# Twenty of the 31 taps of one channel half of a depthwise convolution computed on GpSimd instead of VectorE

## What is computed

```python
glu  = a * sigmoid(b)                 # a, b: two of the parts of h @ w_in, 256 channels each
conv = _dwconv(glu, conv_a_w, conv_a_b)   # 31 taps, padding 15 on both sides
y    = silu(layer_norm(conv, ln_a_g, ln_a_b))
```

## Time and profile before

| what | us |
|---|---|
| median of three runs | 2552.96 |
| the profiled execution | 2552.17 |
| its span on the core | 2550.5 |
| TensorE busy | 2430.3 (95% of the span) |
| VectorE busy | 1620.2 (64%) |
| ScalarE busy | 991.7 (39%) |
| GpSimd busy | 30.6 (1%) |
| mixer loop of layer 0, taps of line 2119 | 1646.6 to 1738.9 |
| mixer loop of layer 1, taps of line 2119 | 2237.2 to 2311.0 |

### The profile page before, as it was taken

How to read it: one execution, slowest core, us unless ns; L and a number is a source line. 1 busy time by engine, 2 the same in 40 slices (tenths; PEclk the granted TensorE clock), 3 DMA queues, 4 the chain that set the end, 5 groups by cost and what they waited for, 6 DMA issues and landing times. The chain is left out here.

```text
span 2550.5 us, 30749 instructions
## 1 busy us (share of the span) xinstructions
PE 2430.3 (95%) x12146; PEld 1941.0 (76%) x12146; DVE 1620.2 (64%) x2607; ACT 991.7 (39%) x1532; POOL 30.6 (1%) x64
## 2 busy tenths in 40 slices
PE   7999999999999999999999998998999999878997
PEld 3878877866686888886668996766788888757997
DVE  7776665444476886766457676487775454576664
ACT  2322322255523322224445444465331232455543
POOL 0000000010000000000000000000000000000000
PEclk9999999999999999999899999999999999988999
DMA  8355445531341444442314552211335443222653
GB/s 319 102 210 188 163 145 185 219 144 68 147 171 62 153 174 159 148 148 84 119 39 143 191 179 92 82 62 54 121 135 198 157 173 124 79 83 83 199 179 120
DMA packets 95802, 357.15 MB, mean 140 GB/s; under 512 B 10969, under 2 KB 11353, under 8 KB 93353
## 3 DMA queue, kind: packets, MB, share of 16 engines
q1 hardware_dynamic: 93082, 339.37, 38.3%
q0 software_dynamic: 2576, 15.82, 1.7%
HBM read 349.90 MB, written 5.24 MB: 139 GB/s over the span
## 5 line engine op out<-in xcount | busy, mean ns | idle before, releaser
L1546 DVE TENSOR_TENSOR w_lo<-raw,w_hi 128x1024 fp32r<-128x1024 f32 (+1 forms) x456 | 543.4, 1209 | 354.3 <-ACT w_hi L1026 353.9
L1026 ACT ACTIVATE w_hi<-raw 128x1024 fp32r<-128x1024 f32 (+1 forms) x456 | 461.6, 1041 | 539.5 <-PE PS L527 528.9
L527 PE MATMUL PS<-h_hi,w_hi 128*128 128x512 f32 (+1 forms) x1528 | 524.5, 343 | 19.4 <-DVE h_lo L1898 9.2
L527 PE MATMUL PS<-h_lo,w_hi 128*128 128x512 f32 (+1 forms) x1528 | 521.2, 341 | 0.0
L527 PE MATMUL PS<-h_hi,w_lo 128*128 128x512 f32 (+1 forms) x1528 | 520.5, 341 | 0.0
L527 PEld LDWEIGHTS PS<-h_hi,w_hi 128*128 128x128 f32 x1528 | 287.7, 188 | 64.3 <-issue 12.9
L527 PEld LDWEIGHTS PS<-h_hi,w_lo 128*128 128x128 f32 x1528 | 287.7, 188 | 35.9
L527 PEld LDWEIGHTS PS<-h_lo,w_hi 128*128 128x128 f32 x1528 | 287.9, 188 | 34.7 <-issue 0.2
L527 PE MATMUL PS<-hid_hi,w_hi 128*128 128x512 f32 (+1 forms) x864 | 292.3, 338 | 0.0
L527 PE MATMUL PS<-hid_lo,w_hi 128*128 128x512 f32 (+1 forms) x864 | 292.2, 338 | 0.0
L527 PE MATMUL PS<-hid_hi,w_lo 128*128 128x512 f32 (+1 forms) x864 | 292.2, 338 | 0.0
(11 more groups left out here) (341 smaller groups left out, 3440.4 us busy)
## 6 DMA issues: line engine op xcount, KB each, us to landing
raw<-in_weights SPq DMA_DIRECT2D x434, 512.0 KB, 4.6
ada_ring<-in_ada SPq DMA_DIRECT2D x176, 512.0 KB, 3.8
raw<-in_weights SPq DMA_DIRECT2D x22, 384.0 KB, 4.0
qk<-in_ada SPq DMA_DIRECT2D x4, 1024.0 KB, 10.9
xv<-in_ada SPq DMA_DIRECT2D x4, 1024.0 KB, 12.9
m_hi<-h_spill POOLq DMA_DIRECT2D x4, 1024.0 KB, 8.1
wgt<-in_x SPq DMA_DIRECT2D x2, 1024.0 KB, 22.5
h_spill<-h_hi POOLq DMA_DIRECT2D x1, 2048.0 KB, 9.1
```

The lines of the kernel that those rows point to most:

```text
L527: mm = pe.matmul(out, a, b, start=(k == 0 and i == 0), stop=(k == ph.k_tiles - 1 and i == 2))
L1026: act.activation(w_hi[:, s, 0:w], raw[:, s, 0:w], ACT.Copy).then_inc(sem("w_hi"), 1)
L1546: dve.tensor_tensor(w_lo[:, s, 0:w], raw[:, s, 0:w], w_hi[:, s, 0:w].bitcast(F32), ALU.subtract)\
```

## The change

On VectorE only taps 0 to 10 of half 0 stay, with all 31 of half 1: 42 taps, no longer alternating. Taps 11 to 30 of half 0 go to GpSimd, which has no fused form here: the first is one multiplication into a temporary, each further one is a multiplication into a second temporary and an addition, 20 multiplications and 19 additions in each layer, each waiting for the one before it. VectorE adds the sum of GpSimd to its own in one instruction, `both_parts`, in step 13, and TensorE in step 14 waits for both halves before the first multiplication. The taps for each step become 3 + 1 in steps with a slot and 5 in the others.

```diff
+DVE_TAPS = 11
 def conv_taps():
-    first = [(k, 0) for k in range(12)]
-    both = [(k, j) for i in range(19) for k, j in ((i, 1), (12 + i, 0))]
-    return first + both + [(k, 1) for k in range(19, 31)]
+    return [(k, 0) for k in range(DVE_TAPS)] + [(k, 1) for k in range(31)]
...
         # GpSimd, in each layer behind its DMAs
+                seqs, r = (slice(0, 2), slice(0, T)) if l == 0 else (slice(1, 2), LAT)
+                wide = lambda i: TMP[:, i, r].rearrange("p (s n) -> p s n", n=CTX)
+                pool.wait_ge(sem("glu_made"), 2 * l + 1)
+                for k in range(DVE_TAPS, 31):
+                    at = V2["conv_a_w_2"] + (31 * l + k) * 2
+                    src, first = glu[:, 0, seqs, k:k + CTX], k == DVE_TAPS
+                    if k > DVE_TAPS + 1:
+                        pool.wait_ge(sem("pool_sum"), (29 - DVE_TAPS) * l + k - DVE_TAPS - 1)
+                    pool.tensor_scalar(wide(2 if first else 3), src, vec2[:, at:at + 1], None, ALU.mult).then_inc(sem("pool_tap"), 1)
+                    pool.wait_ge(sem("pool_tap"), (31 - DVE_TAPS) * l + k - DVE_TAPS + 1)
+                    if not first:
+                        ins = pool.tensor_tensor(wide(2), wide(2), wide(3), ALU.add)
+                        ins.then_inc(sem("pool_sum" if k < 30 else "pool_taps"), 1)
...
         # TensorE, step 14
                         pe.wait_ge(sem("sg_used"), 2 * (l + 1))
+                        pe.wait_ge(sem("conv_in"), 2 * (l + 1))
                         sum_two(lambda j: conv[:, j, r], "conv_in")
...
         # VectorE
+                def both_parts():
+                    dve.wait_ge(sem("tap"), (30 + DVE_TAPS) * l + last[0])
+                    dve.wait_ge(sem("pool_taps"), l + 1)
+                    dve.tensor_tensor(conv[:, 0, r], conv[:, 0, r], TMP[:, 2, r], ALU.add).then_inc(sem("conv_in"), 1)
...
                         maxima(at)
-                        convolve(4 if i >= 4 else 0)
+                        convolve(3 if i >= 4 else 0)
                         factors(at)
                         convolve(1 if i >= 4 else 0)
                         differences(at)
...
                     if i >= 4:
-                        convolve((1 if i in SCORE_AT[l] else 6) if i < 13 else len(taps))
+                        convolve((0 if i in SCORE_AT[l] else 5) if i < 13 else len(taps))
+                    if i == 13:
+                        both_parts()
```

More of the change, by code:

```diff
@@ L2105, in gated_linear_unit @@
                     dve.tensor_tensor(glu[:, j, seqs, 15:15 + CTX], segments(z[:, j, r]), segments(z[:, 2 + j, r]), ALU.mult)\
-                        .then_inc(sem("dve_chain"), 1)
-                    dve.wait_ge(sem("dve_chain"), chained())
+                        .then_inc(sem("glu_made"), 1)
+                    dve.wait_ge(sem("glu_made"), 2 * l + j + 1)
                 def convolve(count):
@@ L2117, in convolve @@
                         else:
-                            dve.wait_ge(sem("tap"), 60 * l + last[j])
+                            dve.wait_ge(sem("tap"), (30 + DVE_TAPS) * l + last[j])
                             ins = dve.scalar_tensor_tensor(out=dst, in0=src, scalar=w, in1=dst, op0=ALU.mult, op1=ALU.add)
```

## The result

The changed kernel takes 2566.17 us (median of 5, 2563.50 to 2572.73) against 2552.96 us (5 runs, 2551.41 to 2555.33): a ratio of 1.0058, 95% interval 1.0042 to 1.0074. It is slower by some 13 to 15 us. The profiled execution took 2566.05 us with a span of 2564.3, 13.8 more than before.

What follows compares the result with a forecast made beforehand. TensorE, busy 95% of the span, was taken to bound the kernel, with VectorE nearly full in both mixer loops. Layer 0 at +4.6 and layer 1 at +0.9 made +5.5 us: 2558.5 us forecast, range 2549 to 2568.

Steps and rivals of the forecast that it cites:

- the forecast proper: Whole kernel: the central case, in which VectorE and GpSimd take turns at SBUF, 2555.5 to 2565 us; chance 0.42.
- The sum without interference: Both layers: gain in TensorE's gaps from 20 fewer VectorE taps if nothing interfered, 1.8 us in layer 0, -2.9 in all.
- The wait of `both_parts`, costed at nothing: Step 13: GpSimd's taps, 28 to 37 us, end before it even at twice that, so the new wait costs nothing.
- the third rival: GpSimd's taps take 72 us or more in layer 0; if past step 13, TensorE stops; 2568 us, chance 0.13.
- The price of a turn: VectorE instructions with two SBUF inputs meeting GpSimd's: 0.4 us at 512 columns (0.30 to 0.61), 0.25 at 256.
- The lag of VectorE into TensorE: Layer 0: VectorE's lag at the differences, less time in hand, makes TensorE 3.05 us late in step 6, 5.2 in step 8.
- the term of layer 0, "+4.6": Mixer loop of layer 0: TensorE 5.2 us late by step 8, less 0.4 and 0.2 in steps 10 and 14.
- Layer 1: Mixer loop of layer 1: step 5 pays 2.0 us less 0.5, then -0.6 in step 14, +0.9 in all.
- my mark of 6 or more: Layer 1, step 5: sign of the forecast, TensorE's wait of 4.86 us growing to 6 or more.
- The engines don't block each other: Rival: no or hardly any blocking, 2550.0 us, up to 2548; decided by a layer 0 step 4 wait under 1.87; chance 0.23.
- Blocking at the low price: Rival: turns at 0.30 us (0.1 in layer 1), additions holding VectorE no longer than multiplications; 2554.5 us, chance 0.22.
- GpSimd becomes the bound: Rival: GpSimd comes past step 13, `both_parts` waits and TensorE stops; or longer gaps cost layer 1 clock; 2568 us, chance 0.13.

Runs made afterwards that it cites:

- the run without GpSimd: Changed kernel with GpSimd's 39 instructions of each layer and the wait for them left out; ratio 0.9990 to the kernel before, median 2553.06 us.
- filled waits: Changed kernel with dummy products on TensorE in front of its long waits in the mixer stages; 2557.07 us, ratio 1.0005 to the kernel before.
- the run with additions only: Changed kernel with GpSimd's multiplications but the first of each layer left out, its 19 additions kept; ratio 1.0034 to the kernel before, median 2566.05 us.
- with memsets: Changed kernel with each of GpSimd's 39 instructions of a layer replaced by a memset of the same columns; ratio 0.9995 to the kernel before, median 2553.22 us.
- the kernel with 3 + 1 + 2 taps: Kernel before, 62 taps on VectorE, one tap of each slot step moved from before the reciprocals to the step's end; 2552.50 us, ratio 0.9989.

## Why the prediction was right, and where it was off

The direction and the range held (2558.5 forecast, 2549 to 2568, measured 2566.17), for the reason given: VectorE and GpSimd take turns when both read SBUF, and TensorE waits for the differences in steps 4, 6 and 8. The size did not: +5.5 us against +13.2, which is outside the 2555.5 to 2565 of the forecast proper. That the range held is in part luck: its upper end stood for turns at 0.61 us each, or for a GpSimd that comes late, and neither happened. The clock, which the sum left out, took up that room.

*What VectorE saves.* The sum without interference gave -2.9; the run without GpSimd gave -2.5. By TensorE's waits the part of layer 0 is right, 1.4 us less (8.3 to 6.9) where I had 1.8: steps 4, 8 and 10 as I had them, step 14 not. The agreement of the totals is luck beyond that. In layer 1 the idle time fell by 0.2 us and not by 1.1, and the stages moved by more than the waits, by +2.7 and -4.2 us, with the clock (0.98 to 0.94, 0.81 to 0.84).

*The wait of `both_parts`, costed at nothing.* Right, GpSimd had 39 us in hand. But the durations were not: I worked out 0.61 us for a multiplication of 512 columns from the selects, and it takes 1.57. GpSimd worked for 72 us in layer 0 and not for the 50 to 60 of the sum, so it was at work in step 10 too, where I had put a gain of 0.4 (which the run without GpSimd has) and the wait grew by 1.6. The 72 us, to 1712, were in the third rival's text, with the right remark that this is still in time.

*The price of a turn.* I took 0.4 as the mean over both kinds. Over 39 instructions that is 15.6 us in layer 0; 19 additions at 0.76 to 0.95 and 20 multiplications at 0.10 to 0.15 make 16 to 21, and VectorE's busy time rose by 18.3 over the run without GpSimd, a mean of 0.47. The mean was nearly right by luck: the multiplication was put too dear (0.40), and the addition came out near the top of its range (0.82) or over it.

*The lag of VectorE into TensorE.* Waits of 4.15, 0.44 and 3.27 us in steps 4, 6 and 8 where I had TensorE 5.2 us late by step 8: they sum to 7.9 against 2.7 before, so this term is right. With 1.6 more in step 10 and 0.2 more in step 14, where I had 0.6 less, the idle time grew by 7.0 us instead of 4.6.

*The step that failed* is the term of layer 0, "+4.6", which held only waits. The other 7.1 us of that stage are the clock, 0.92 instead of 0.98, that I named only in the third rival and only for layer 1. It was the larger miss. The clock is lower just behind the longer waits (0.92, 0.66 and 0.81 where it was 1.00), and with filled waits it is 1.00 and the ratio 1.0005 instead of 1.0058. How much of the 7.1 us is due to the change is open: a profile without GpSimd had 0.94 too, only 3.0 us of matmul time less, and the ratios put some 6 us of the whole loss, not clear of noise, on the clock.

*Layer 1.* Forecast +0.9, measured -1.3. The wait that I named grew from 4.86 to 7.73, in line with my mark of 6 or more. I had GpSimd done by 2265, but it worked until 2289.7, and a second wait grew from 3.55 to 5.20. The idle time grew by 3.9, but the clock in the stage was higher, 0.85 against 0.81. Why it is higher with more idle time is left open; it came out the same in the kernel with GpSimd in layer 1 only.

*The rivals.* "The engines don't block each other" falls by the step-4 wait, the mark that I had set for it. "Blocking at the low price" had said that additions hold VectorE no longer than multiplications; a VectorE instruction beside them pays six to seven times as much. "GpSimd becomes the bound" did not happen, though its 2568 is nearest to the time. That is luck: the clock that it names is that of layer 1, which rose.

## What to carry to other kernels

Work moved from VectorE to GpSimd need not be taken off VectorE if both read SBUF: here each GpSimd addition of 512 columns made a VectorE instruction beside it 0.76 to 0.95 us longer, more than a tap costs VectorE itself (0.75). Look first at what waits for VectorE: moving one tap a step behind the critical instruction won as much as taking 20 away (0.9989 and 0.9990). And where a wait of TensorE grows, look at the clock as well as the wait: here it fell in layer 0 and rose in layer 1.

## What the runs showed that I had not expected

- GpSimd's multiplication by a column of weights takes 1.57 us for 512 columns and 0.92 for 256 (the first of each layer in the run with additions only), longer than its addition of two tiles at its shortest (1.27) and three times a memset (0.53). VectorE hardly pays for it.
- A VectorE instruction with a single SBUF input takes turns too: the first tap of a half (`tensor_scalar`, 512 columns) took 1.53 us beside additions, instead of 0.54. It took 0.70 beside memsets, which taps and splits don't feel at all, and kept its 0.54 beside multiplications. The rows are of the runs with additions only and with memsets, one instruction each:

```profile
1648.79 1.53 DVE L2129 TENSOR_SCALAR conv<-glu,vec 128x512 f32<-128x512 f32 x1
...
1645.93 0.70 DVE L2131 TENSOR_SCALAR conv<-glu,vec 128x512 f32<-128x512 f32 x1
```

- Dummy products in TensorE's waits brought some 6 us back in the kernel with 3 + 1 + 2 taps (0.9989 to 0.9964) and 8 in the one without GpSimd's work (0.9990 to 0.9960), in a program that is 95% busy on TensorE by the page.
